# Modulating the Hyena input by feature block over four tiles, the first spectrum on VectorE alone, the gate rows in the last residue, and grouped-query squares on ScalarE

## The chip, the cores and the metric

One core of a Trainium2 chip runs the whole program. The metric is device time in microseconds, median of three runs.

## What is computed

Two layers of a mixer over 1024 sample tokens and 128 prompt tokens of width 1024. The part of the reference that the change touches:

```python
mod = silu(c) @ ada_w + ada_b            # c_ctx for the prompt token tile
shift, scale, gate = split(mod, 3)
h = rmsnorm(x, norm_pre) * (1.0 + scale) + shift
z = h @ w_in                             # 3*256 columns of it are the Hyena input
gq = rmsnorm(g_q, gqa_q_norm); gk = rmsnorm(g_k, gqa_k_norm)   # per head of 64
# Hyena: two long convolutions by real FFT of filters computed by a small sine network
spec = rfft(u, 2n) * rfft(filt, 2n); y = irfft(spec)[:n] + u * bias
out = x + gate * rmsnorm(o @ w_out, norm_post)
```

All is float32.

## The kernel before, in words

Everything is scheduled by hand, engine by engine, with semaphores. A token tile is 128 tokens; tiles 0 to 7 are sample, tile 8 (`NT`) prompt; `TT` is 9. An engine's instructions run in program order. PSUM has eight banks. `claim` (line 671) makes TensorE wait until the last job in a bank was drained; `K.next()` (line 299) deals banks in turn, and `K.restart` sets the turn, so that the turn is not the same in both layers. `full` and `emptied` are the states of a job's bank. An fp32 matmul leaves two records in the trace, a transpose one.

Per layer the stage around the change runs so:

1. For o = 1 and then o = 0, TensorE makes nine filter products (`f3`), then the forward transform in four residues `a0` in `FE_ORDER` (2, 0, 1, 3), two products `p` each, eight jobs `FE`, with the six column blocks of the conditioning (`ada`) laid between. For o = 0 it first makes 16 two-column products (`modT`, one job) that turn the conditioning into columns; behind the residues come four `gate_row` products.
2. ScalarE drains the `FE` jobs into the buffer B2. VectorE (`butterfly`, line 1864) and GpSimd (`butterfly`, line 2496) share the radix-4 step from B2 through B3 to HS: VectorE makes sums and rows 0 and 2, GpSimd the differences and rows 1 and 3. The result for o = 1 goes out by DMA (`spectrum_kept`, line 555), after a wait for GpSimd (line 553). ScalarE drains the `FE` jobs of o = 0 only after the first spectrum is made, since B2 is used again; after some of them it squares a tile of x (`square`, line 1367).
3. VectorE makes the modulation columns (`modulation`, line 1873), normalizes six tiles (`normalize`, line 1892, with an inverse root on GpSimd in its middle), multiplies the gate rows (`gate_rows`), adds the bias, and modulates.
4. TensorE turns x tile by tile (`x_turned`, line 786): two banks of four transposes a tile. ScalarE modulates the lower four feature blocks, VectorE the upper four (`modulate`, line 1899), four instructions of 128 columns each per tile. `hyena_input(f, i)` (line 804) multiplies feature block f by token part i (512, 512 and 128 tokens), eight matmuls each; for f = 0 it waits until all tiles of the part are modulated. Order: tiles 0 to 4, input (0,0), tiles 5 and 6, (1,0), tiles 7 and 8, (0,1), (0,2), and then f = 1 to 5. The ring for x has six places; the DMAs for tiles 6 to 8 start when tiles 0 to 2 are turned.
5. After VectorE made the second spectrum (`butterfly` for o = 0), ScalarE drains the input jobs into the place of B2.

In the grouped-query stage each tile passes through projection (TensorE), a copy to SBUF (ScalarE, line 1765), `head_sums` (VectorE, line 2341: squares, sums, scaled), an inverse root on GpSimd, rotary and `split` (VectorE), and transposes (`parts_turned`, TensorE). The last gate product of the stage goes into bank 7 (line 1299), and the attention's `take_bank` waits for its drain (line 974).

## Time and profile before

| | us |
|---|---|
| median of 3 runs | 2381.16 |
| lowest, highest | 2380.28, 2382.45 |
| the profiled execution | 2381.92 |
| its span | 2380.1 |

TensorE is busy for 93% of the span, VectorE for 55%, ScalarE for 40%, GpSimd for 13%. The mean granted clock of TensorE is 0.993 of full speed. The chain of work that ended last follows the profile back for a few microseconds only, so the order of the work is read from the timelines of the engines, and the idle time before each entry, with what ended it, in brackets. Entries of a timeline merge instructions of the same kind; lengths overlap by some hundredths of a microsecond.

### The profile page before, as it was taken

How to read it: one execution, taken by the hardware profiler on the slowest of the kernel's cores; microseconds unless marked ns; L12 is line 12 of the kernel's file. 1: busy time of each engine (PE TensorE's matmuls, PEld its weight loads, DVE VectorE, ACT ScalarE, POOL GpSimd, SP SyncE). 2: the span in 40 equal slices, each digit the busy share in tenths (PEclk: the TensorE clock that was granted, in tenths of full speed). 3: DMA queues.
4: the chain of work that ended last, by engine and by line, in shares of the span. 5: the costliest groups of instructions: out<-in, count | busy, mean ns of one | idle time of the engine just before them, and what ended most of it. 6: DMA issues, size and time to landing. Idle time of an engine off the chain costs nothing. (4 is left out here: it accounts for less than half of the span.)

```text
span 2380.1 us, 36768 instructions
## 1 busy us (share of the span) xinstructions
PE 2223.0 (93%) x14648; PEld 1605.8 (67%) x14648; DVE 1315.8 (55%) x2450; ACT 961.9 (40%) x1957; POOL 311.3 (13%) x458
## 2 busy tenths in 40 slices
PE   6999999899999998989999999999999999889898
PEld 4556865685677776864866577657856777768657
DVE  3642764564856466583546247545656654855732
ACT  2422113554255266483224221135532652745721
POOL 0410000000200013022314000010011000220323
PEclk9999999999999999999999999999999999999999
DMA  7600100100020000113276001001001100002022
GB/s 238 250 36 29 58 19 1 55 1 15 1 79 2 4 5 7 37 37 134 80 244 238 30 1 58 18 21 35 2 15 38 42 2 7 1 7 73 2 90 88
DMA packets 75042, 124.96 MB, mean 53 GB/s; under 512 B 25778, under 2 KB 38962, under 8 KB 73332
## 3 DMA queue, kind: packets, MB, share of 16 engines
q1 hardware_dynamic: 73816, 121.64, 14.8%
q8 instruction: 118, 1.93, 0.3%
q10 hardware_dynamic: 1056, 0.96, 0.2%
q14 instruction: 52, 0.43, 0.1%
HBM read 105.38 MB, written 17.20 MB: 52 GB/s over the span
## 5 line engine op out<-in xcount | busy, mean ns | idle before, releaser
L677 PE MATMUL psum<-arena 128*32 128x256 f32 (+9 forms) x9168 | 1381.2, 383 | 57.2 <-ACT arena L1352 11.8
L677 PEld LDWEIGHTS psum<-arena 128*32 128x32 f32 (+3 forms) x9168 | 879.5, 149 | 492.2 <-issue 360.0
L681 PE MATMUL psum<-ident,arena 128*128 128x128 f32 (+1 forms) x2248 | 333.3, 278 | 67.5 <-ACT arena L1631 31.1
L1819 DVE TENSOR_TENSOR arena<-arena 128x32 f32<-128x32 f32 (+10 forms) x686 | 307.8, 494 | 102.3 <-ACT arena L1492 42.6
L681 PEld LDWEIGHTS psum<-ident,arena 128*128 128x128 f32 (+1 forms) x2248 | 251.7, 140 | 153.5 <-issue 103.2
L677 PE MATMUL psum<-k_parts,q_parts 96*128 96x384 f32 (+2 forms) x1000 | 267.6, 363 | 11.9 <-ACT arena L1527 6.0
L2113 DVE TENSOR_REDUCE st<-psum 128x1 f32<-128x1152 f32 (+1 forms) x144 | 178.0, 1237 | 48.7 <-PE psum L677 48.4
L2208 DVE TENSOR_REDUCE st<-psum 128x1 f32<-128x1152 f32 (+1 forms) x144 | 174.7, 1236 | 49.0 <-PE psum L677 48.6
L677 PEld LDWEIGHTS psum<-k_parts,q_parts 96*128 96x128 f32 (+1 forms) x1000 | 168.4, 191 | 29.4 <-issue 10.9
L1819 DVE TENSOR_TENSOR arena<-psum,arena 128x512 f32<-128x512 f32 (+2 forms) x104 | 57.1, 564 | 228.1 <-PE psum L677 228.1
L1527 ACT ACTIVATE arena<-psum,st 128x1152 f32<-128x1152 f32 (+1 forms) x144 | 162.4, 1128 | 49.1 <-DVE st L2113 41.4
L1542 ACT COPY arena<-psum 128x512 f32<-128x512 f32 (+1 forms) x244 | 101.9, 433 | 186.1 <-PE psum L681 186.0
L1617 ACT ACTIVATE arena<-psum,st 128x1152 f32<-128x1152 f32 (+1 forms) x144 | 162.3, 1128 | 26.4 <-DVE st L2208 25.4
L2454 POOL TENSOR_TENSOR arena<-arena 128x512 f32<-128x512 f32 (+4 forms) x74 | 135.8, 1846 | 192.2 <-ACT arena L1362 82.5
L2454 POOL TENSOR_TENSOR st<-st,minus 128x1 f32<-128x1 f32 x72 | 42.3, 588 | 721.0 <-ACT arena L1617 721.0
L2127 DVE COPY arena<-psum 128x512 f32<-128x512 f32 (+1 forms) x156 | 93.7, 613 | 28.9 <-PE psum L681 28.9
L1631 ACT COPY arena<-psum 128x512 f32<-128x512 f32 (+1 forms) x200 | 90.2, 469 | 41.5 <-PE psum L681 40.6
L2218 DVE SCALAR_TENSOR_TENSOR arena<-arena,st 128x1152 f32<-128x1152 f32 (+1 forms) x72 | 96.0, 1334 | 11.7 <-POOL st L2454 11.7
L1980 DVE SCALAR_TENSOR_TENSOR arena<-arena,hcw 128x1024 f32<-128x1024 f32 x24 | 30.8, 1285 | 124.2 <-ACT arena L1446 123.8
L2454 POOL TENSOR_TENSOR st<-st,mhalf 128x1 f32<-128x1 f32 (+2 forms) x72 | 60.6, 841 | 242.3 <-DVE st L1824 135.5
L1580 ACT ACTIVATE arena<-psum 128x512 f32<-128x512 f32 x36 | 21.5, 598 | 171.9 <-PE psum L677 171.9
L1741 ACT CAST q_parts<-psum 96x512 fp32r<-96x512 f32 (+1 forms) x54 | 31.5, 584 | 117.8 <-PE psum L681 117.8
(160 smaller groups left out, 1945.6 us busy)
## 6 DMA issues: line engine op xcount, KB each, us to landing
arena<-in_ada_w SPq DMA_DIRECT2D x12, 2048.0 KB, 8.7
arena<-in_w_in SPq DMA_DIRECT2D x10, 2048.0 KB, 8.2
arena<-in_x SPq DMA_DIRECT2D x18, 512.0 KB, 5.7
out_xs<-arena SPq DMA_DIRECT2D x18, 512.0 KB, 2.6
arena<-out_xs SPq DMA_DIRECT2D x18, 512.0 KB, 5.7
arena<-in_w_out SPq DMA_DIRECT2D x4, 2048.0 KB, 8.0
spectrum_kept<-arena SPq DMA_DIRECT2D x2, 2304.0 KB, 8.4
arena<-spectrum_kept SPq DMA_DIRECT2D x2, 2304.0 KB, 8.8
```

Of the source, the lines that this page charges most:

```text
L677: return nc.tensor.matmul(out, lhsT, rhs, start=start, stop=stop)
L681: return nc.tensor.transpose(out, src, ident[0:n, 0:n])
L1527: nc.scalar.activation(at(buf, nk, w), psum[:, 512 * b0:512 * (b0 + nk)].rearrange("p (c n) -> p c n", c=nk)[:, :, 0:w], ACT.Exp, bias=st[ ...
L1542: nc.scalar.copy(at(SLOTS[grp] + slot(grp, u) * 1152 + 512 * j, nk * P), bank[b][:, 0:nk * P]).then_inc(*S.up("turned_scalar", (grp, number)))
L1617: nc.scalar.activation(at(buf, nk, w), psum[:, 512 * b0:512 * (b0 + nk)].rearrange("p (c n) -> p c n", c=nk)[:, :, 0:w], ACT.Exp, bias=st[ ...
L1631: nc.scalar.copy(at(SLOTS[grp] + slot(grp, u) * 1152 + 512 * j, nk * P), bank[b][:, 0:nk * P]).then_inc(*S.up("turned_scalar", (grp, number)))
L1819: return nc.vector.tensor_tensor(out, a, b, op)
L2113: nc.vector.tensor_reduce(st[:, 16 + x % 4:17 + x % 4], psum[:, 512 * b0:512 * (b0 + nk)].rearrange("p (c n) -> p c n", c=nk)[:, :, 0:w], ...
L2127: nc.vector.tensor_copy(at(SLOTS[grp] + slot(grp, u) * 1152 + 512 * j, nk * P), bank[b][:, 0:nk * P]).then_inc(*S.up("turned_vector", (grp ...
L2208: nc.vector.tensor_reduce(st[:, 16 + x % 4:17 + x % 4], psum[:, 512 * b0:512 * (b0 + nk)].rearrange("p (c n) -> p c n", c=nk)[:, :, 0:w], ...
L2218: nc.vector.scalar_tensor_tensor(p0, p1, c, p0, ALU.mult, ALU.add).then_inc(*S.up("mixed", (grp, u)))
L2454: return nc.gpsimd.tensor_tensor(out, a, b, op)
```

## The change

1. The 16 two-column products are laid one by one behind the matmuls of the first two residues of o = 0 (`modulation_column`). The four gate row products move from behind the last residue to between its two products.
2. For o = 1 VectorE makes the whole radix-4 step (`spectrum_butterfly`, eight instructions); GpSimd keeps its part for o = 0 only. The DMA of the spectrum waits for VectorE.
3. Tiles 0 to 3 are turned by feature block: bank k takes block k of all four tiles, and one instruction of 512 columns modulates it (even k ScalarE, odd k VectorE). `hyena_input(0, 0)` waits block by block. Tiles 4, 5 and 6, 7 go in pairs, two blocks to a bank, 256 columns an instruction. Five tiles are normalized before the gate rows, tile 5 after the modulation of the first four, tiles 6 and 7 behind the bias. The DMAs for tiles 6 to 8 all start when the four tiles are turned. Input products take banks 0, 1, 6, 7 where they took 2, 3, 6, 7.
4. In the grouped-query stage ScalarE squares the projection from PSUM between its two copies, and VectorE no longer does. The last gate product takes bank 6.

```diff
@@ -550,7 +551,7 @@
 sp.wait_ge(*K.emptied(("f3", 0, FILTER_ORDER[-1])))
 for t in range(RING):
     load_x(t)
-sp.wait_ge(*S.at("butterfly_pool", ("F", 1)))
+sp.wait_ge(*S.at("spectrum_turned"))
 sp.wait_ge(*S.at("spectrum1_made"))
 sp.dma_start(spectrum_kept, at(HS, 4608)).then_inc(*S.up("spectrum1_kept", None, 16))
@@ -563,7 +564,7 @@
 sp.dma_start(gates_kept, at(SGH, 2 * D)).then_inc(*S.up("gate_rows_kept", None, 16))
 for t in range(RING, TT):
-    sp.wait_ge(*K.full(("xT", t - RING, 1)))
+    sp.wait_ge(*K.full(("xT_four", KD - 1)))
     load_x(t)
 sp.wait_ge(*K.full(("xT", NT, 1)))
 load(at(TI, 4096), I["tab_i"], "inverse_table")
...
@@ -722,6 +723,22 @@
 mod = at(A_MOD, 3072)
+def modulation_column(m, columns):
+    last = mm(columns[:, 2 * m:2 * m + 2], mod[:, m * P:(m + 1) * P], sel[:, :, 0])
+    if m == 2 * KD - 1:
+        last.then_inc(*K.done(("modT",)))
+def gate_row_products():
+    pe.wait_ge(*S.at("ada_biased", 5))
+    for s in range(2):
+        for half in range(2):
+            ps = claim(("gate_row", s, half), K.next())
+            mm(ps[:, :], sel[:, s, :], mod[:, 2 * D + half * 512:2 * D + (half + 1) * 512]
+               ).then_inc(*K.done(("gate_row", s, half)))
 tf = at(TF, 2 * NT, 2, P)
 ti = at(TI, 2 * NT, 2, P)
 eo = at(EO, TT, 3, GW)
...
@@ -766,7 +780,13 @@
                 for i, (a, kind) in enumerate(terms):
                     last = mm(ps[:, ri * GW:(ri + 1) * GW], tf[:, 2 * a + p, ri, :],
                               eo[:, a, kind, :], i == 0, i == len(terms) - 1)
+                    if o == 0 and turn < 2 and (ri, i) != (1, len(terms) - 1):
+                        modulation_column(8 * turn + 4 * p + 2 * ri + i, columns)
             last.then_inc(*K.done(("FE", o, a0, p)))
+            if o == 0 and turn < 2:
+                modulation_column(8 * turn + 4 * p + 3, columns)
+            if o == 0 and (turn, p) == (3, 0):
+                gate_row_products()
         if turn == 1:
             pe.wait_ge(*S.at("filter_folded", (o, NT)))
             ps = claim(("FEp", o), K.next())
@@ -775,13 +795,26 @@
             last.then_inc(*K.done(("FEp", o)))
     if o:
         ada(3)
-    else:
-        pe.wait_ge(*S.at("ada_biased", 5))
-        for s in range(2):
-            for half in range(2):
-                ps = claim(("gate_row", s, half), K.next())
-                mm(ps[:, :], sel[:, s, :], mod[:, 2 * D + half * 512:2 * D + (half + 1) * 512]
-                   ).then_inc(*K.done(("gate_row", s, half)))
+def four_turned():
+    for t in FOUR:
+        pe.wait_ge(*S.at("x_normed", t))
+    for k in range(KD):
+        ps = claim(("xT_four", k), [k])
+        for t in FOUR:
+            last = flip(ps[:, t * P:(t + 1) * P], at(XN[t] + k * P, P))
+        last.then_inc(*K.done(("xT_four", k)))
...
+def pair_turned(n, banks):
+    for t in PAIRED[n]:
+        pe.wait_ge(*S.at("x_normed", t))
+    for j in range(4):
+        ps = claim(("xT_pair", n, j), banks[j])
+        for i in range(2):
+            for a, t in enumerate(PAIRED[n]):
+                last = flip(ps[:, (2 * i + a) * P:(2 * i + a + 1) * P],
+                            at(XN[t % RING] + (2 * j + i) * P, P))
+        last.then_inc(*K.done(("xT_pair", n, j)))
 def x_turned(t, banks):
...
@@ -805,25 +838,27 @@
     c, (tok, n) = "hy0" if f < 4 else "hy1", PARTS[i]
     weights(c)
-    if f < 1:
-        for t in range(tok // P, (tok + n) // P):
-            for half in range(2):
-                pe.wait_ge(*K.emptied(("xT", t, half)))
+    if f < 1 and i == 1:
+        for pair in range(2):
+            for j in range(4):
+                pe.wait_ge(*K.emptied(("xT_pair", pair, j)))
+    if f < 1 and i == 2:
+        for half in range(2):
+            pe.wait_ge(*K.emptied(("xT", NT, half)))
     ps = claim(("u", f, i), banks)
     for k in range(KD):
+        if f < 1 and i == 0:
+            pe.wait_ge(*K.emptied(("xT_four", k)))
         last = mm(ps[:, 0:n], W[:, SLOT[c, 0], k, (f % 4) * P:(f % 4 + 1) * P],
                   hT[:, k, tok:tok + n], k == 0, k == KD - 1)
     last.then_inc(*K.done(("u", f, i)))
-for t in range(4):
-    x_turned(t, ([2 * t], [2 * t + 1]))
-x_turned(4, ([0], [1]))
-hyena_input(0, 0, [2])
-x_turned(5, ([4], [5]))
-x_turned(6, ([6], [7]))
-hyena_input(1, 0, [3])
-x_turned(7, ([0], [1]))
-x_turned(8, ([4], [5]))
+four_turned()
+hyena_input(0, 0, [0])
+pair_turned(0, ([2], [3], [4], [5]))
+hyena_input(1, 0, [1])
+pair_turned(1, ([6], [7], [2], [3]))
+x_turned(NT, ([4], [5]))
 hyena_input(0, 1, [6])
...
@@ -971,7 +1006,7 @@
         for j in range(pieces(grp, u)):
             turned_by[piece_number(grp, u, j)] = f"turned_{piece_engine(grp, u, j)}"
-    side = {7: K.emptied(("gate", "gqa", *LAST_GATE["gqa"]))} if grp == "gqa" else {}
+    side = {6: K.emptied(("gate", "gqa", *LAST_GATE["gqa"]))} if grp == "gqa" else {}
     def take_bank(b, released):
@@ -1296,7 +1331,7 @@
     parts_turned(grp, TT)
     if grp == "gqa":
         gate("gqa", "gqa_gate", 0, *GQA_GATES[4], K.next())
-    gate(grp[:4], vg, vg0, *LAST_GATE[grp], [7])
+    gate(grp[:4], vg, vg0, *LAST_GATE[grp], [6 if grp == "gqa" else 7])
     if grp != "diff1":
         pe.wait_ge(*S.at(f"{grp[:4]}_values"))
...
-                                    bias=mcol[:, k, s:s + 1])
-    last.then_inc(*K.drained(job))
-    if t >= 3 and t + 3 < TT:
-        square(t + 3)
+def modulate(job, k, s, tok, c, n):
+    return nc.scalar.activation(hT[:, k, tok:tok + n], B(job)[:, c:c + n], ACT.Identity,
+                                scale=mcol[:, KD + k, s:s + 1], bias=mcol[:, k, s:s + 1])
+for k in range(0, KD, 2):
+    act.wait_ge(*K.full(("xT_four", k)))
+    modulate(("xT_four", k), k, 0, 0, 0, 512).then_inc(*K.drained(("xT_four", k)))
+square(6)
+square(7)
+for n in range(2):
+    for j in range(2):
+        job = ("xT_pair", n, j)
+        act.wait_ge(*K.full(job))
+        modulate(job, 2 * j, 0, 512 + n * 256, 0, 256)
+        modulate(job, 2 * j + 1, 0, 512 + n * 256, 256, 256).then_inc(*K.drained(job))
+    if n == 0:
+        square(8)
+job = ("xT", NT, 0)
+act.wait_ge(*K.full(job))
+for k in range(4):
+    last = modulate(job, k, 1, NT * P, k * P, P)
+last.then_inc(*K.drained(job))
 act.wait_ge(*S.at("butterfly_vector", ("F", 0)))
...
@@ -1764,6 +1812,10 @@
             nz = 384 if grp == "gqa" else 256
             ins = nc.scalar.copy(at(z, nz), B(job)[:, 0:nz])
             if grp == "gqa":
+                if i >= 1:
+                    act.wait_ge(*S.at("variance", ("heads", i - 1)))
+                nc.scalar.activation(at(SQ, 384), B(job)[:, 0:384], ACT.Square)
                 ins = nc.scalar.copy(at(VV + key_tile(i) * GW, P), B(job)[:, 384:512])
             ins.then_inc(*K.drained(job))
         if grp == "gqa" and i + GQA_SPLIT + 1 < TT:
...
@@ -1870,6 +1922,19 @@
     tt(X[:, 0, :], M[:, 0, :], M[:, 1, :], ALU.add)
     link(tt(X[:, 2, :], M[:, 0, :], M[:, 1, :], ALU.subtract), "butterfly_vector", key)
+def spectrum_butterfly(src, mid, dst):
+    E, M, X = at(src, 4, D), at(mid, 4, D), at(dst, 4, D)
+    R, Y = at(mid, 4, 2, 2, GW), at(dst, 4, 2, 2, GW)
+    link(tt(M[:, 0:2, :], E[:, 0:2, :], E[:, 2:4, :], ALU.add), "butterfly_sums", ("F", 1))
+    link(tt(M[:, 2:4, :], E[:, 0:2, :], E[:, 2:4, :], ALU.subtract), "spectrum_diffs")
+    tt(X[:, 0, :], M[:, 0, :], M[:, 1, :], ALU.add)
+    tt(X[:, 2, :], M[:, 0, :], M[:, 1, :], ALU.subtract)
+    tt(Y[:, 1, :, 0, :], R[:, 2, :, 0, :], R[:, 3, :, 1, :], ALU.add)
+    tt(Y[:, 1, :, 1, :], R[:, 2, :, 1, :], R[:, 3, :, 0, :], ALU.subtract)
+    tt(Y[:, 3, :, 0, :], R[:, 2, :, 0, :], R[:, 3, :, 1, :], ALU.subtract)
+    link(tt(Y[:, 3, :, 1, :], R[:, 2, :, 1, :], R[:, 3, :, 0, :], ALU.add), "spectrum_turned")
 def modulation():
...
+def modulate_four():
+    for k in range(1, KD, 2):
+        v.wait_ge(*K.full(("xT_four", k)))
+        modulate(("xT_four", k), k, 0, 0, 0, 512).then_inc(*K.drained(("xT_four", k)))
+def modulate_pair(n):
+    for j in range(2, 4):
+        job = ("xT_pair", n, j)
+        v.wait_ge(*K.full(job))
+        modulate(job, 2 * j, 0, 512 + n * 256, 0, 256)
+        modulate(job, 2 * j + 1, 0, 512 + n * 256, 256, 256).then_inc(*K.drained(job))
+def modulate_prompt():
+    job = ("xT", NT, 1)
     v.wait_ge(*K.full(job))
     for k in range(4):
-        last = nc.vector.tensor_scalar(hT[:, 4 + k, t * P:(t + 1) * P], B(job)[:, k * P:(k + 1) * P],
-                                       mcol[:, KD + 4 + k, s:s + 1], mcol[:, 4 + k, s:s + 1],
-                                       ALU.mult, ALU.add)
+        last = modulate(job, 4 + k, 1, NT * P, k * P, P)
     last.then_inc(*K.drained(job))
...
@@ -1936,9 +2018,12 @@
 for o in (1, 0):
     if o == 0:
         modulation()
-        for t in range(RING):
+        for t in range(RING - 1):
             normalize(t)
         gate_rows()
+        v.wait_ge(*K.emptied(("gate_row", 1, 1)))
+        modulate_four()
+        normalize(RING - 1)
     for a0 in range(4):
         for p in range(2):
...
@@ -1949,13 +2034,17 @@
         link(nc.vector.scalar_tensor_tensor(E[:, 0, p, 0, :], bias, 1.0 / N_SAMPLE, E[:, 0, p, 0, :],
                                             ALU.mult, ALU.add), "bias_added", (o, p))
     if o == 0:
-        v.wait_ge(*K.emptied(("gate_row", 1, 1)))
-        for t in range(TT):
-            modulate(t)
-            if t >= 4 and t + 2 < TT:
-                normalize(t + 2)
+        normalize(6)
+        normalize(7)
+        modulate_pair(0)
+        normalize(8)
+        modulate_pair(1)
+        modulate_prompt()
         v.wait_ge(*S.at("spectrum1_kept"))
-    butterfly(("F", o), B2, B3, HS, -1)
+    if o:
+        spectrum_butterfly(B2, B3, HS)
+    else:
+        butterfly(("F", o), B2, B3, HS, -1)
     v.wait_ge(*K.emptied(("FEp", o)))
     nc.vector.scalar_tensor_tensor(at(HS + 4096, GW), bias, 1.0 / N_PROMPT, at(B2 + 4096, GW),
...
@@ -2341,8 +2430,7 @@
 def head_sums(i):
     v.wait_ge(*K.emptied(("proj", "gqa", i)))
-    z, r6 = ZB + (i % 2) * WC, st[:, 8 * (i % 2):8 * (i % 2) + 6]
-    link(tt(at(SQ, 384), at(z, 384), at(z, 384), ALU.mult))
+    r6 = st[:, 8 * (i % 2):8 * (i % 2) + 6]
     link(nc.vector.tensor_reduce(r6, at(SQ, 6, 64), AX.X, ALU.add))
     nc.vector.tensor_scalar(r6, r6, 1.0 / 64, EPS, ALU.mult, ALU.add).then_inc(*S.up("variance", ("heads", i)))
...
@@ -2531,13 +2619,12 @@
             inverse_root(("x", t), st[:, t:t + 1])
             if t == 1:
                 bias_ada(5)
-    for a0 in range(4):
-        for p in range(2):
-            pool.wait_ge(*K.emptied(("FE", o, a0, p)))
-    pool.wait_ge(*S.at("bias_added", (o, 1)))
-    if o == 0:
-        pool.wait_ge(*S.at("spectrum1_kept"))
-    butterfly(("F", o), B2, B3, HS, -1, range(RING, TT) if o == 0 else ())
+for a0 in range(4):
+    for p in range(2):
+        pool.wait_ge(*K.emptied(("FE", 0, a0, p)))
+pool.wait_ge(*S.at("bias_added", (0, 1)))
+pool.wait_ge(*S.at("spectrum1_kept"))
+butterfly(("F", 0), B2, B3, HS, -1, range(RING, TT))
```

## Rows read from the trace of the kernel before

**Rows 1.** The page, first part: busy time, share of the span and instructions of each engine.

```profile
PE 2223.0 (93%) x14648; PEld 1605.8 (67%) x14648; DVE 1315.8 (55%) x2450; ACT 961.9 (40%) x1957; POOL 311.3 (13%) x458
```

**Rows 2.** Waits of TensorE over the whole span: who waited for whom, us, times, longest.

```profile
PE psum L681 <- DVE split_buf L1819: 8.7, 10, 1.2
```

**Rows 3.** Timeline of TensorE, layer 0: start us, us, engine, line, operation, idle before it.

```profile
69.85 3.73 PE L677 MATMUL psum<-sel,arena 128*128 128x2 f32 x32
...
73.45 13.52 PE L677 MATMUL psum<-arena 128*128 128x256 f32 x68
...
88.10 10.63 PE L677 MATMUL psum<-arena 128*128 128x256 f32 x48 [1.13 <-DVE mcol L1879]
...
98.56 3.60 PE L677 MATMUL psum<-arena,sel 128*128 128x512 f32 x8
...
102.00 3.66 PE L681 MATMUL psum<-ident,arena 128*128 128x128 f32 x32
...
110.66 9.81 PE L677 MATMUL psum<-arena 128*128 128x512 f32 x16 [3.37 <-DVE arena L1904]
...
122.06 7.03 PE L677 MATMUL psum<-arena 128*128 128x512 f32 x16
...
131.62 17.54 PE L677 MATMUL psum<-arena 128*128 128x512 f32 x64 [0.78 <-DVE arena L1904]
```

**Rows 4.** Timeline of TensorE, layer 1, the same stage.

```profile
1246.25 25.40 PE L677 MATMUL psum<-arena 128*128 128x256 f32 x116
...
1276.27 4.88 PE L681 MATMUL psum<-ident,arena 128*128 128x128 f32 x40 [1.18 <-DVE arena L1819]
...
1283.59 8.74 PE L677 MATMUL psum<-arena 128*128 128x512 f32 x16 [2.44 <-DVE arena L1904]
...
1303.47 8.89 PE L677 MATMUL psum<-arena 128*128 128x512 f32 x32 [0.78 <-DVE arena L1904]
...
1314.99 8.89 PE L677 MATMUL psum<-arena 128*128 128x512 f32 x32 [2.63 <-ACT arena L1439]
```

**Rows 5.** Windows: length, busy us of five engines, granted clock, DMA share, GB/s.

```profile
1246.20:1250.00 3.80, 3.80 (x11) 3.12 (x12) 3.73 (x5) 0.95 (x3) 1.98 (x1) 0.59 0.44 117
...
113.00:116.00 3.00, 3.00 (x5) 1.09 (x4) 1.91 (x2) 2.67 (x8) 1.78 (x2) 0.50 0.14 53
```

**Rows 6.** Timeline of VectorE, layer 0.

```profile
75.24 9.96 DVE L1819 TENSOR_TENSOR arena<-arena 128x2048 f32<-128x2048 f32 x3
...
91.52 0.76 DVE L1896 TENSOR_SCALAR arena<-arena,st 128x1024 f32<-128x1024 f32 x1 [0.67 <-POOL st L2454]
...
101.92 2.48 DVE L1819 TENSOR_TENSOR arena<-psum,arena 128x512 f32<-128x512 f32 x4
...
127.23 1.75 DVE L1896 TENSOR_SCALAR arena<-arena,st 128x1024 f32<-128x1024 f32 x1 [0.66 <-POOL st L2454]
...
132.56 4.68 DVE L1819 TENSOR_TENSOR arena<-arena 128x2048 f32<-128x2048 f32 x3
```

**Rows 7.** Timeline of GpSimd, layer 0.

```profile
75.38 14.97 POOL L2454 TENSOR_TENSOR arena<-arena 128x2048 f32<-128x2048 f32 x6 [10.94 <-DVE arena L1949]
```

**Rows 8.** Timeline of ScalarE, layer 0.

```profile
92.06 0.61 ACT L1411 ACTIVATE arena<-psum 128x512 f32<-128x512 f32 x1
...
112.09 1.06 ACT L1371 ACTIVATE arena<-arena 128x1024 f32<-128x1024 f32 x1 [1.92 <-DMA arena<-in_x]
```

**Rows 9.** Timeline of TensorE, grouped-query stage of layer 0.

```profile
594.02 0.47 PE L677 MATMUL psum<-gqa_w_high,gqa_h_high 128*128 128x512 f32 x1 [1.50 <-DVE gqa_w_low L1819]
...
614.65 1.09 PE L681 MATMUL psum<-ident,split_buf 128*128 128x128 f32 x8 [0.77 <-DVE split_buf L1819]
...
669.68 2.02 PE L677 MATMUL psum<-arena 128*128 128x128 f32 x16 [0.98 <-ACT k_parts L1749]
```

**Rows 10.** Timeline of VectorE, grouped-query stage of layer 0.

```profile
614.51 0.55 DVE L1819 TENSOR_TENSOR arena<-arena 128x384 f32<-128x384 f32 x1
```

**Rows 11.** Timeline of ScalarE, grouped-query stage of layer 0.

```profile
616.35 0.49 ACT L1765 COPY arena<-psum 128x384 f32<-128x384 f32 x1
```

19 lines of the change are left out of this document (6 added, 13 removed).

## Prediction

> **What bounds the kernel now.** The page's busy line comes first: TensorE is busy for 93% of the span, nobody else for more than 55% [rows 1]. So a change is worth what it takes out of TensorE's idle time, what it gives back of TensorE's clock, and nothing else; work moved between the other engines counts only where TensorE waits for it. The second view is therefore TensorE's timeline through the stage, with the wait in brackets, once per layer [rows 3, 4]. The reader sees a queue that runs without a gap through the filter transform and then breaks up: it waits 1.13 us for the modulation columns in layer 0 and 1.18 us for a drained gate row in layer 1, 3.37 and 2.44 us for the modulation of the first four tiles, 0.78 us for that of the last ones, and in layer 1 another 2.63 us for a bank that ScalarE has to drain. The third view is the windows with the granted clock [rows 5]: two places of this stage run at or near 1.2 GHz and not 2.4. Last come VectorE, GpSimd and ScalarE at the same times [rows 6 to 8], to see what is late next, and the same three views in the grouped-query stage [rows 2, 9 to 11].
>
> **First spectrum on VectorE alone.** Before, VectorE's three instructions take 9.96 us while GpSimd's six run for 14.97 us beside them [rows 6, 7]; the same three take 4.68 us where GpSimd is silent at 132.56 [rows 6]. The new eight instructions are the 2048-column sum twice, two of 1024 columns and four of 512. The old three are one sum and two of 1024, so four units of 1024 columns took 4.68 us: 1.17 us a unit. The new work is eight units, 9.4 us, with GpSimd silent. The two small copies behind it also ran beside GpSimd before. I expect the first spectrum 2 to 2.5 us sooner (bounds 0 to 3), and the columns with it. TensorE reaches the bank of the columns at 86.97 (73.45 + 13.52) and waits 1.13 us [rows 3]: that wait goes. In layer 1 there was none, as TensorE was slower there by the clock. Two DMAs of weights and one of the spectrum start about 3.4 us sooner, since GpSimd's end is no longer awaited. Gain: 1.1 us, layer 0.
>
> **Columns laid into the residues.** The 16 products took 3.73 us for 32 records [rows 3], 0.117 us each, which is a weight load and not the two columns. Laid between matmuls of 256 columns each still brings two weight loads, of which one at most hides behind its neighbour. I put the change at nothing, bounds -1.9 and +1.9 us a layer. What it may change is the clock. In layer 1 the 3.8 us right behind the block of columns were granted 0.59, so mostly 1.2 GHz [rows 5], and the 116 records took 25.40 us where layer 0 took 13.52 + 10.63 = 24.15 [rows 3, 4]. What TensorE did before it fell was a stretch of 32 weight loads with almost no columns; spread out, there is no such stretch. I take 1.25 us back in layer 1 (bounds 0 and 1.25).
>
> **Gate rows in the last residue.** The same 3.60 us of TensorE [rows 3], free of cost, but VectorE's 2.48 us for the gate rows [rows 6] now runs beside the last product instead of behind everything. The 1.18 us wait in layer 1 [rows 4] was for a gate row's bank; by counting the banks dealt, in layer 1 the gate rows now hold 6, 7, 0, 1 and the last product 2, all drained when the turned block reaches them. By walking the queues VectorE ends the gate rows about 0.8 us before the last product ends: cover enough, and without it up to 1 us a layer comes back. The gate rows wait for the last conditioning block, which GpSimd completes behind its second inverse root; walking the queues puts that about 2 us early.
>
> **Four tiles by block.** The 32 transposes take 3.66 us [rows 3], 0.114 us each, so a block of four is full every 0.46 us. An engine drains one in about 0.61 us (ScalarE) or 0.62 us (VectorE, 2.48 / 4) [rows 6, 8], and each gets every second block, one in 0.92 us: the engines keep up. The first input product uses a block every 7.03 / 8 = 0.88 us [rows 3], so it can start right behind the transposes. Before, it stood behind 40 transposes and the 3.37 us wait, and then ran at 1.2 GHz: the window shows 0.50, and the product took 9.81 us, not 7.03 [rows 3, 5]. In layer 1: 2.44 us and 8.74 us [rows 4].
>
> New TensorE line from the start of the transposes to input (0,1): 32 transposes 3.6, product 6.9, 16 transposes 1.8, product 6.9, 16 and 8 transposes 2.8, together 22.0 us, start to start. I add 0.5 us for the last modulation, as VectorE must normalize tile 8 and modulate two banks before (0,1). That makes 22.5. Before it was 131.62 - 102.00 = 29.62 us in layer 0 [rows 3]: gain 7.1. In layer 1 it was 1303.47 - 1276.27 = 27.20 [rows 4]: gain 4.7, and with the 1.18 us wait and the 1.25 us of clock 7.1. Layer 0 with its 1.1 us makes 8.2.
>
> **What is late next.** Tile 6 must be normalized before the second pair is turned, 19.2 us into the new line (3.6 + 6.9 + 1.8 + 6.9). Its DMA landed at 112.0 before (ScalarE waited 1.92 us for it [rows 8]); that is 11 us into the new line, and the queue ahead of it starts 3.4 us sooner. Squares of tiles 6 and 7 take 1.06 us each. Normalizing costs VectorE 0.76 us alone and 1.75 us beside GpSimd's part of the second spectrum [rows 6]. With 1.75 each and GpSimd's root between, both are done about 17.3 us into the line. Cover: 1.9 us. ScalarE now has its squares ahead of the first pair's modulation, which no transposed bank is short of.
>
> **The bank in layer 1.** The 2.63 us wait at 1314.99 [rows 4] is input (1,1) claiming bank 3, which input (1,0) held. Now (1,0) takes bank 1 and bank 3 holds a turned pair long drained. The wait goes. In layer 0 (1,1) now claims bank 0 with input (0,0) in it, undrained until the second spectrum is made; the same walk has that due about 1.6 us before. Gain 2.6 us in layer 1 (bounds 1 and 2.6). Behind this stage TensorE's queue has no gap that depends on an absolute time, so the shift stays.
>
> **Grouped-query squares.** Per tile TensorE waits 0.77 us for VectorE's split [rows 9], ten such waits of 8.7 us in all [rows 2]. VectorE's loop runs without slack but for the root, and it loses one instruction of 0.55 us [rows 10], 0.59 with its gap. Five waits a layer; the stage's first wait, 1.50 us for the rounded weights [rows 9], shrinks by 0.2 only, as ScalarE now squares before it lets VectorE go. VectorE's shift grows by 0.59 a tile and TensorE takes it over but for about 0.2 us that remains a tile: 4.35 - 1.2 = 3.1 us a layer, 6.3 in all (bounds 0 and 8.7). ScalarE's new instruction is like its copy, 0.49 us [rows 11], and ScalarE idles for over 3 us in each tile. It waits for the variance of the tile before, which VectorE makes right behind the split whose transposes ScalarE drains first: no wait, and only this tile's two copies would be queued behind it.
>
> **Last gate in bank 6.** Bank 7 held the last transposed keys, and TensorE waited 0.98 us [rows 9]; bank 6 was drained a tile ago. Twice 0.98: 2.0 us.
>
> **Sum.** 8.2 + 7.1 + 2.6 + 6.3 + 2.0 = 26.2 us. The profiled execution had 2381.92 us around its span of 2380.1, so it would have 2355.7; it lies 0.76 above the median of 2381.16, which gives 2355.0.
>
> **A rule beside the rows.** VectorE's three instructions took twice as long beside GpSimd [rows 6, 7]. The Trainium skill (SBUF — State Buffer, Who interferes with whom) says that a VectorE instruction with two SBUF inputs, or one in a two-port mode, and a GpSimd instruction lock each other out for a whole instruction. By that rule, the trace agrees, the new spectrum is safe, but the normalizing of tiles 6 to 8 is not: it now stands in the middle of GpSimd's second spectrum. That is the third rival below.
>
> **The rivals.**
> *Transposes cool the clock* (15%). The 32 transposes in a row are 3.66 us of short work, and both falls of the clock came near short work. Against it: the clock was still full during them. Then the first product costs 8.74 to 9.81 us as now, +1.7 to +2.8 us in both layers: about 2359.5.
> *The squares were not the bound* (8%). ScalarE's longer drain takes the place of VectorE's instruction: none of the 6.3 us, 2361.3.
> *VectorE late for the tail* (12%). Each of tiles 6 to 8 waits for one more GpSimd instruction. A 512-column one is some 1.3 us (14.97 us holds the 2048-column one, four such and a small one, slowed); three are 3.9 us, and the 0.5 us at input (0,1) grows by all of it: +7.8 us over two layers, 2362.8.
> *The clock is lost over the whole stage* (3%, the one that ends slower). Thin products in the residues and short transposes keep TensorE at 1.2 GHz, where work takes twice as long. The two residues with columns are 10.6 us of work, the transposes and first product 10.5. If all of that ran slow in both layers it costs 42 us: 2397. It decides from 13.1 us of slow work a layer. Against it: layer 0 ran the densest block of columns and what followed with no fall at all.
>
> **How the numbers follow.** The forecast holds 62%, its own range 2351 to 2358. With the second to fourth cases up to 2363 no more than 2 in 10 are left out. Below, 2350 takes in TensorE losing all waits for the split and hidden column loads in part. A difference of 0.2% (4.8 us) is about what a measurement of this kernel can tell from no change. Every case but the last is faster by more: 0.95; 0.02 for a sum of mishaps within it, 0.03 slower.
>
> **What would show it.** After: no wait for the columns; transposes x32 followed at once by the first product in 7.03 us at a clock of 1.0; input (0,1) 22.5 us behind the first transpose; no wait for ScalarE's drain in front of (1,1) in layer 1; VectorE's first spectrum in 9 to 9.5 us; waits for the split down from 8.7 to about 2.4 us; none of 0.98 us before the last gate. Wrong would be a wait of over 1 us for a normalized tile, a first product of over 8 us, or a per-tile wait for the split still near 0.77.

## The result and the profile after

| | before | after |
|---|---|---|
| median, us | 2381.8 (2380.28 to 2386.9) | 2358.14 (2356.43 to 2358.81) |
| the profiled execution | 2381.92 | 2357.67 |
| its span | 2380.1 | 2355.9 |
| mean granted clock | 0.993 | 0.993 |

The ratio of the changed kernel to the one before, on one chip, is 0.9892 with a 95% interval of 0.988 to 0.9905: about 1.1% faster, 2358.14 us where 2355.0 was forecast.

The page first, as before: busy time, share and instructions of each engine. TensorE is busy for 4.5 us less than in [rows 1], with as many instructions; the other 20 us of the 24.2 us of span are idle time that went.

```profile
PE 2218.5 (94%) x14648; PEld 1604.3 (68%) x14648; DVE 1295.3 (55%) x2402; ACT 959.2 (41%) x1935; POOL 281.4 (12%) x448
```

TensorE's timeline in layer 0 (start us, us, engine, line, operation, idle before it). It answers [rows 3]. The 80.02 row is the last of the 16 two-column products, each between two records of 128x256.

```profile
80.02 0.28 PE L678 MATMUL psum<-sel,arena 128*128 128x2 f32 x2
80.16 13.52 PE L678 MATMUL psum<-arena 128*128 128x256 f32 x68
93.52 3.60 PE L678 MATMUL psum<-arena,sel 128*128 128x512 f32 x8
96.95 3.62 PE L678 MATMUL psum<-arena 128*128 128x256 f32 x16
100.40 3.66 PE L682 MATMUL psum<-ident,arena 128*128 128x128 f32 x32
103.89 7.03 PE L678 MATMUL psum<-arena 128*128 128x512 f32 x16
...
112.51 7.03 PE L678 MATMUL psum<-arena 128*128 128x512 f32 x16
119.38 2.92 PE L682 MATMUL psum<-ident,arena 128*128 128x128 f32 x24
123.21 17.54 PE L678 MATMUL psum<-arena 128*128 128x512 f32 x64 [0.91 <-DVE arena L1966]
```

No column wait stands inside the 68 records, the gate rows stand ahead of the last 16 records of the transform, the 32 transposes are followed by the first product at once, and this takes 7.03 us where it took 9.81. From the first transpose to input (0,1) it is 123.21 - 100.40 = 22.81 us, where it was 29.62. One wait is left, 0.91 us.

The same stage in layer 1, answering [rows 4]: again 1287.53 - 1264.68 = 22.85 us, where it was 27.20, and 64 records in one row where the wait for ScalarE had cut them into 32 and 32.

```profile
1264.68 3.69 PE L682 MATMUL psum<-ident,arena 128*128 128x128 f32 x32
1268.21 7.03 PE L678 MATMUL psum<-arena 128*128 128x512 f32 x16
...
1287.53 17.54 PE L678 MATMUL psum<-arena 128*128 128x512 f32 x64 [0.91 <-DVE arena L1966]
```

Windows over the first product of layer 0 and over what follows the columns in layer 1 (length, busy us of five engines, granted clock, DMA share, GB/s). Where [rows 5] show 0.50 and 0.59, both are now at the upper level, 2.4 GHz:

```profile
104.00:111.00 7.00, 7.00 (x20) 3.12 (x19) 2.57 (x7) 2.62 (x5) 4.12 (x2) 1.00 0.95 372
1244.50:1248.30 3.80, 3.80 (x26) 1.88 (x25) 3.77 (x5) 0.00 (x0) 0.00 (x0) 1.00 1.02 419
```

VectorE, GpSimd and ScalarE in layer 0, the same columns as the timeline of TensorE; these rows answer [rows 6 to 8]:

```profile
75.75 9.42 DVE L1871 TENSOR_TENSOR arena<-arena 128x2048 f32<-128x2048 f32 x8
...
105.63 0.75 DVE L1961 TENSOR_SCALAR arena<-arena,st 128x1024 f32<-128x1024 f32 x1 [0.66 <-POOL st L2542]
...
112.63 1.75 DVE L1961 TENSOR_SCALAR arena<-arena,st 128x1024 f32<-128x1024 f32 x1 [2.29 <-POOL st L2542]
...
115.11 1.75 DVE L1961 TENSOR_SCALAR arena<-arena,st 128x1024 f32<-128x1024 f32 x1 [0.67 <-POOL st L2542]
...
119.39 1.76 DVE L1961 TENSOR_SCALAR arena<-arena,st 128x1024 f32<-128x1024 f32 x1 [0.67 <-POOL st L2542]
121.07 3.17 DVE L1966 TENSOR_SCALAR arena<-psum,mcol 128x256 f32<-128x256 f32 x8
```

```profile
107.43 4.53 POOL L2542 TENSOR_TENSOR arena<-arena 128x2048 f32<-128x2048 f32 x1 [1.84 <-DVE arena L2034]
112.04 0.55 POOL L2542 TENSOR_TENSOR st<-st,mhalf 128x1 f32<-128x1 f32 x1
```

```profile
108.93 1.06 ACT L1406 ACTIVATE arena<-arena 128x1024 f32<-128x1024 f32 x1 [4.02 <-DMA arena<-in_x]
```

The first spectrum takes 9.42 us for its eight instructions. The x tile 6 is there at 108.9, 3.1 us sooner than at 112.0 before. Its inverse root on GpSimd (112.04) stands behind GpSimd's first instruction of the second spectrum, 4.53 us from 107.43 on, so VectorE waits 2.29 us for it, and VectorE's normalizing takes 1.75 us beside GpSimd, where that of tile 5 took 0.75 with GpSimd silent (105.63).

Waits of TensorE in both grouped-query stages (who waited for whom, us, times, longest), answering [rows 2] and the first of [rows 9]:

```profile
PE psum L682 <- DVE split_buf L1871: 2.0, 6, 0.4
...
PE psum L678 <- DVE gqa_w_low L1871: 2.6, 2, 1.3
```

**Where the 24 us went.** Starts of the same instruction, before and after, give the gain of each stage:

| stage | forecast | measured, two layers |
|---|---|---|
| Hyena, layer 0, to input (0,1) | 8.2 | 8.2 (1.4 ahead of the transposes, 6.8 behind) |
| Hyena, layer 1, to input (0,1) | 7.1 | 7.4 (3.0 ahead, 4.4 behind) |
| bank before input (1,1), layer 1 | 2.6 | 2.9 |
| grouped-query squares | 6.3 | 7.8 |
| last gate | 2.0 | 2.5 |
| sum | 26.2 | 28.8 |
| span | | 24.2 |

Every term came at its size or above it, and yet the span fell by 24.2 us only. The missing 4.6 us stand outside all changed stages. Below are the windows at one of the places where the shift of the two traces jumps, here by 1.7 us: first of the changed kernel, then of a second profiled execution of the same kernel (experiment 1).

```profile
770.00:775.00 5.00, 3.85 (x46) 2.43 (x36) 1.76 (x7) 1.16 (x5) 0.00 (x0) 0.92 0.00 0
775.00:780.00 5.00, 5.00 (x19) 4.13 (x19) 0.00 (x0) 0.23 (x1) 0.00 (x0) 0.74 0.01 3
```

```profile
770.00:775.00 5.00, 3.85 (x43) 2.50 (x35) 1.76 (x7) 1.16 (x5) 0.00 (x0) 1.00 0.00 0
775.00:780.00 5.00, 5.00 (x25) 4.38 (x24) 0.00 (x0) 0.27 (x1) 0.00 (x0) 1.00 0.02 3
```

TensorE was busy to the same extent in both up to 775; in the one its clock fell, and in the next 5 us it did 19 records where the other did 25.

**The bracket is not the whole price of a wait.** Three terms came above their waits, and starts show why. In a queue that runs, neighbouring records overlap: the transposes above end at 100.40 + 3.66 = 104.06, and the product starts at 103.89. A wait takes this overlap of 0.16 us away, and the second record behind it comes another 0.03 to 0.10 us late. So the bracket of 0.98 us before the last gate [rows 9] was worth 1.24 us of start to start, that of 1.13 us for the columns [rows 3] 1.4, and that of 2.63 us for the bank [rows 4] 2.9.

### The profile page after: what moved, and what is told of

The parts are those of the page before. It is cut to its first block and busy times, and to the rows that moved or that the text cites. A ratio compares the mean times of both kernels' runs of the same rounds, so it can differ in the third digit from the quotient of the medians.

```text
span 2355.9 us, 36664 instructions
## 1 busy us (share of the span) xinstructions
PE 2218.5 (94%) x14648; PEld 1604.3 (68%) x14648; DVE 1295.3 (55%) x2402; ACT 959.2 (41%) x1935; POOL 281.4 (12%) x448
## 5 line engine op out<-in xcount | busy, mean ns | idle before, releaser
L1871 DVE TENSOR_TENSOR arena<-arena 128x256 f32<-128x256 f32 (+9 forms) x678 | 298.4, 487 | 84.4 <-ACT arena L1540 42.6
L2542 POOL TENSOR_TENSOR arena<-arena 128x512 f32<-128x512 f32 (+4 forms) x64 | 108.9, 1710 | 177.9 <-ACT arena L1397 95.1
L2307 DVE SCALAR_TENSOR_TENSOR arena<-arena,st 128x1152 f32<-128x1152 f32 (+1 forms) x72 | 96.0, 1334 | 11.8 <-POOL st L2542 11.8
```

Of the source, the lines that this page charges most:

```text
L1871: return nc.vector.tensor_tensor(out, a, b, op)
L2307: nc.vector.scalar_tensor_tensor(p0, p1, c, p0, ALU.mult, ALU.add).then_inc(*S.up("mixed", (grp, u)))
L2542: return nc.gpsimd.tensor_tensor(out, a, b, op)
```

## The experiments

Two measures are used. The median is that of four executions, of ten in experiments 10 and 11. Experiments 1 to 4, 5 to 8 and 9 to 11 ran on three different chips; each ratio is to the kernel before on the same chip, so a ratio compares better across these groups than a median. Beside it stands the profiled span *at full clock*, an estimate: the lost clock is the sum over all 5-us windows of 5 us x (1 - granted clock), and 0.85 of it is taken off the span. The 0.85 comes from two pairs of executions of an identical kernel: spans of 2355.9 and 2351.3 us with 17.1 and 11.8 us lost, and of 2380.1 and 2385.4 with 18.6 and 25.2. It gives 2341.4 and 2341.3 for the one pair, 2364.3 and 2363.9 for the other, where the spans themselves differ by 5 us. That these agree tests nothing, since the 0.85 was taken from them; the timelines of the experiments below do, and differ from the number by up to 2 us. So a part worth 1 to 5 us, which the medians can't tell, is read from the timeline, with this number beside it.

| kernel | median, us | ratio to before | span at full clock | against changed |
|---|---|---|---|---|
| before | 2381.8 | 1 | 2364.3 | +22.9 |
| changed | 2358.14 | 0.9892 | 2341.4 | |
| 1 changed, again | 2356.01 | 0.9888 (0.9871 to 0.9904) | 2341.3 | -0.1 |
| 2 squares on VectorE | 2365.87 | 0.992 (0.9906 to 0.9935) | 2349.1 | +7.7 |
| 3 bank 3 for (1,0) | 2360.41 | 0.9901 (0.9886 to 0.9916) | 2344.6 | +3.2 |
| 4 columns in a block | 2358.05 | 0.9892 (0.9877 to 0.9907) | 2341.2 | -0.2 |
| 5 tile by tile | 2373.81 | 0.9949 (0.9933 to 0.9966) | 2357.5 | +16.1 |
| 6 gate rows last | 2355.34 | 0.9871 (0.9857 to 0.9886) | 2340.8 | -0.6 |
| 7 spectrum shared | 2357.85 | 0.988 (0.9866 to 0.9895) | 2342.7 | +1.3 |
| 8 last gate in bank 7 | 2357.58 | 0.9884 (0.9869 to 0.9899) | 2344.2 | +2.8 |
| 9 blocks waited for together | 2359.42 | 0.9901 (0.9883 to 0.9918) | 2343.5 | +2.1 |
| 10 part 4 alone | 2379.02 | 0.9981 (0.9969 to 0.9992) | 2353.7 | -10.6 against before |
| 11 before, again | 2386.49 | 1.0004 (0.9992 to 1.0016) | 2363.9 | -0.4 against before |

### 1. The changed kernel again: what are the falls of the clock in the attention?

The theory: the missing 4.6 us are falls that come or stay away from one execution to the next. The rival: the change moved the work so that they come always. No edit.

> The changed kernel once more, unaltered. What is to be told apart: the stages of the change gave back 8.3, 7.5 and 3.1 us in and behind the modulation of layers 0 and 1 and 10.2 us in the two grouped-query stages, 29 in all, but the span fell by 24.2 us; the other 5 us went in the attention stages, in steps of 1.7 us each, at each of which the windows show a granted clock of about 0.5. Theory A (the falls come by chance of phase and move from execution to execution): here the falls outside the changed stages stand at other times than 255, 420, 770, 910, 1060, 1420, 2220, their number differs by one to three, and the time is 2355 to 2360. Theory B (the change itself causes them): they stand at the same places in the same number.

The falls near 420, 770, 1060 and 1420 us are gone and a new one stands at 1580; those near 255, 910, 2220 and 2350 are there again. 11.8 us of clock were lost and not 17.1, and the span is 2351.3 us, 4.6 shorter, of the same kernel. The second span is 28.8 us below that of before, which is the 28.8 of the table. So the gain was made, and in the first profile part of it was covered by falls that need not have come. The rival is answered by the kernel before: its second execution (experiment 11) has falls at 425, 1070 and 1445 us, at the same instructions as those at 420, 1060 and 1420 here, though its first had none of them. But the theory holds in half only. Whether a fall comes changes from one execution to the next; where it can come is much the same in all thirteen traces, as the last section tells.

### 2. The squares back on VectorE

```diff
-                nc.scalar.activation(at(SQ, 384), B(job)[:, 0:384], ACT.Square)
...
+    link(tt(at(SQ, 384), at(z, 384), at(z, 384), ALU.mult))
```

> The changed kernel with the grouped-query squares back on VectorE. My theory: VectorE's loop sets the pace again, each grouped-query stage is 3.9 us longer (I forecast 3.1), waits for the split return to about 8.7 us in all, the time is 6 to 8 us above the changed kernel. Rival (TensorE's own work or ScalarE's drain was the bound, the gain came from the bank of the last gate): under 1 us.

TensorE's waits, as above:

```profile
PE psum L682 <- DVE split_buf L1867: 8.8, 10, 1.3
```

Ten waits of 8.8 us are back where the changed kernel has six of 2.0, and the median rises by 7.7 to 9.9 us over the two medians of the changed kernel. The squares were the bound, and the forecast's 6.3 for this term was too small.

### 3. Input (1,0) in bank 3 again

```diff
-pair_turned(0, ([2], [3], [4], [5]))
-hyena_input(1, 0, [1])
-pair_turned(1, ([6], [7], [2], [3]))
+pair_turned(0, ([2], [1], [4], [5]))
+hyena_input(1, 0, [3])
+pair_turned(1, ([6], [7], [2], [1]))
```

> The changed kernel with banks 1 and 3 exchanged in the Hyena input: input (1,0) sits in bank 3, a turned pair in bank 1. My theory: in layer 1 TensorE waits again before input (1,1) for ScalarE to drain (1,0), 2.6 to 3.1 us, in layer 0 nowhere; the time is 2.6 to 3.1 us above the changed kernel. Rival (the wait went because ScalarE's drain comes earlier, whichever bank): no wait, same time.

TensorE in layer 1, the product of input (1,1):

```profile
1297.32 10.59 PE L678 MATMUL psum<-arena 128*128 128x512 f32 x32 [2.91 <-ACT arena L1487]
```

The wait of [rows 4] is back with 2.91 us (2.63 before), in layer 1 alone; by the starts it costs 3.1 us. Behind it the records took 10.59 us where 32 of them take 8.89: the granted clock was 0.80 in the window from 1295 and 0.85 in that from 1300, so in this execution a fall of the clock stood beside the wait.

### 4. The 16 columns in one block

```diff
+for m in range(2 * KD):
+    modulation_column(m, columns)
...
-                    if o == 0 and turn < 2 and (ri, i) != (1, len(terms) - 1):
-                        modulation_column(8 * turn + 4 * p + 2 * ri + i, columns)
```

> The changed kernel with the 16 two-column products in one block ahead of the residues, as before. My theory: at equal clock the stretch from the first residue to the transposes is within 0.5 us of the changed kernel's 30.6 us; where the clock falls behind the block, as in layer 1 before, it is 1.2 to 1.7 us longer. Rival (laid between, half of the weight loads hide): 1.9 us longer in both layers at a clock of 1.0.

TensorE in layer 0 and in layer 1, and the windows behind the block in layer 1:

```profile
70.06 3.73 PE L678 MATMUL psum<-sel,arena 128*128 128x2 f32 x32
```

```profile
1232.97 4.17 PE L678 MATMUL psum<-sel,arena 128*128 128x2 f32 x32
1237.00 23.35 PE L678 MATMUL psum<-arena 128*128 128x256 f32 x100
```

```profile
1235.00:1240.00 5.00, 5.00 (x23) 4.46 (x23) 4.90 (x9) 1.67 (x4) 0.38 (x1) 0.61 0.07 10
1240.00:1245.00 5.00, 5.00 (x18) 4.11 (x18) 4.93 (x3) 0.00 (x0) 0.00 (x0) 0.71 0.98 373
```

In layer 0 the way from the first of these records to the transposes is 100.80 - 70.06 = 30.74 us. Laid between it is 30.74 us too, from the first record behind the filter products at 69.66 us to 100.40: the columns cost the same in either place. In layer 1 the clock falls right behind the block, as in [rows 5], and the same way takes 34.1 us: 3.4 more, where at most 1.7 was expected. The medians are alike all the same; 3.4 us are within what executions of one kernel differ by. What is shown is the equal price. That spreading the columns *keeps* the clock rests on a count: a fall stands right behind the block of layer 1 in all four traces that have one there (before, before again, experiment 10 and this one), and in none of the nine with the columns spread.

### 5. Turned and modulated tile by tile

`x_turned` for all nine tiles, four modulations of 128 columns a tile and engine, six tiles normalized before the gate rows, the DMAs for tiles 6 to 8 and banks 2 and 3, all as before; the rest as changed.

```diff
-four_turned()
-hyena_input(0, 0, [0])
+for t in range(4):
+    x_turned(t, ([2 * t], [2 * t + 1]))
+x_turned(4, ([0], [1]))
+hyena_input(0, 0, [2])
...
-        for t in range(RING - 1):
+        for t in range(RING):
```

> The changed kernel with the turning and modulation undone: tile by tile, 128 columns an instruction, the old order of normalizing and the old banks 2 and 3; all else stays changed. My theory: the stretch from the first transpose to input (0,1) goes from 22.8 us back to 27 to 30 in both layers, with a wait of 2.4 to 3.4 us before the first product and a fall of the clock in it, and input (1,1) of layer 1 waits 2.6 to 3 us for its bank: 14 us above the changed kernel, about 2371. Rival (with the gate rows and the spectrum sooner, the tile order alone costs little): under 5 us.

TensorE in both layers, and VectorE in layer 1:

```profile
104.49 4.93 PE L682 MATMUL psum<-ident,arena 128*128 128x128 f32 x28 [2.62 <-DVE arena L1836]
112.50 7.11 PE L678 MATMUL psum<-arena 128*128 128x512 f32 x16 [3.08 <-DVE arena L1934]
...
130.75 4.53 PE L678 MATMUL psum<-arena 128*128 128x512 f32 x10 [0.78 <-DVE arena L1934]
```

```profile
1272.82 7.42 PE L682 MATMUL psum<-ident,arena 128*128 128x128 f32 x40 [5.21 <-DVE arena L1836]
```

```profile
1269.31 0.15 DVE L1841 TENSOR_SCALAR st<-st 128x1 f32<-128x1 f32 x1 [4.72 <-ACT arena L1384]
...
1270.80 2.48 DVE L1836 TENSOR_TENSOR arena<-psum,arena 128x512 f32<-128x512 f32 x4
```

The way from the first transpose to input (0,1) is 130.75 - 100.40 = 30.35 us in layer 0, where it is 22.81 with blocks. In layer 1 the same way takes 26.5 us where it is 22.85, behind a wait of 5.21 us, and the bank wait of 2.63 us is back too, since (1,0) is in bank 3 again: 7.5 + 8.9 + 2.6 = 19.0 us, some 4 to 5 of them clock (0.71 granted at 105, 0.69 and 0.63 at 1270 and 1275 us). The medians are 15.7 and 17.8 us above those of the changed kernel, the ratio 0.9949 where it was 0.9892: by far the largest part, where 14 was expected. The wait of 5.21 us has a mechanism of its own: VectorE waits 4.72 us for the square of tile 5, which ScalarE makes only behind the last residue, and drains the gate rows after that (1270.80). Their banks are full as long, and TensorE waits 5.21 us for one. With the gate rows moved forward and the sixth tile left in front of them, their wait, 1.18 us in layer 1 before [rows 4], becomes one of 2.62 us in layer 0 and of 5.21 in layer 1. So by this trace, normalizing five tiles and not six ahead of the gate rows is a needed half of the change. No run has that half alone, so the 14 to 19 us are not shared out between the tile order and the order of normalizing.

### 6. The gate rows behind the last residue

```diff
-            if o == 0 and (turn, p) == (3, 0):
-                gate_row_products()
...
+    else:
+        gate_row_products()
```

> The changed kernel with the gate rows behind the last residue. My theory: in layer 1 the turned blocks 0 and 1 wait for banks that hold gate rows, 1.2 to 2 us, in layer 0 nothing up to 0.7 us: 1 to 3 us in all. Rival (the place of the gate rows does not matter, as the banks are drained in time): no new wait, same time.

VectorE in layer 1, the first and the last of four such rows, then its first modulation:

```profile
1259.11 0.69 DVE L1871 TENSOR_TENSOR arena<-psum,arena 128x512 f32<-128x512 f32 x1 [0.48 <-PE psum L678]
...
1261.69 0.69 DVE L1871 TENSOR_TENSOR arena<-psum,arena 128x512 f32<-128x512 f32 x1 [0.17 <-PE psum L678]
1262.64 3.49 DVE L1966 TENSOR_SCALAR arena<-psum,mcol 128x512 f32<-128x512 f32 x4 [0.26 <-PE psum L682]
```

My theory fell. I had VectorE drain four gate rows in a row of 2.48 us behind the last product; it drains each in 0.69 us while the next, 0.86 us apart, is made, so that only the last one is late, and the first modulation takes up its work 0.26 us after that. The transposes wait for nothing, and from them to input (0,1) it is 22.93 us, as against 22.85. Moving the gate rows into the residue is worth nothing, once VectorE comes to them in time; 2355.34 us is the lowest median of all, but no more below 2356.01 than the same kernel differs from itself.

### 7. The first spectrum shared with GpSimd again

```diff
-    if o:
-        spectrum_butterfly(B2, B3, HS)
-    else:
-        butterfly(("F", o), B2, B3, HS, -1)
+    butterfly(("F", o), B2, B3, HS, -1)
...
```

GpSimd's half and the waits of the DMA and of ScalarE for it are back too.

> The changed kernel with GpSimd sharing the first spectrum again. My theory: the modulation columns come 2.3 us later, so TensorE waits 1 to 1.5 us for them in both layers now (in layer 1 the fallen clock hid it before), x for tiles 6 to 8 lands 3 us later and is still covered: 2 to 3 us in all. Rival (the later DMAs are not covered, tiles 6 and 7 are normalized too late): 5 us or more. Other rival (nothing is waited for): 0.

TensorE in both layers, and VectorE's spectrum and the two small operations behind it in layer 0:

```profile
88.14 7.17 PE L678 MATMUL psum<-arena 128*128 128x256 f32 x32 [1.12 <-DVE mcol L1944]
```

```profile
1253.45 7.17 PE L678 MATMUL psum<-arena 128*128 128x256 f32 x32 [1.12 <-DVE mcol L1944]
```

```profile
75.28 9.96 DVE L1871 TENSOR_TENSOR arena<-arena 128x2048 f32<-128x2048 f32 x3
85.28 1.37 DVE L2046 SCALAR_TENSOR_TENSOR arena<-arena 128x256 f32<-128x256 f32 x1
86.58 1.35 DVE L2048 COPY arena<-arena 128x256 f32<-128x256 f32 x1
```

The wait of 1.13 us for the columns [rows 3] is back, and in layer 1 too, where TensorE is now as fast as in layer 0. By the starts each costs 1.4 us, 2.8 in all, of which the span at full clock shows 1.3. VectorE has fewer instructions and needs longer, 9.96 us, and 1.37 and 1.35 us for two operations that take 0.42 and 0.29 alone. Half the step given to another engine was no relief at all.

### 8. The last gate in bank 7 again

```diff
-gate(grp[:4], vg, vg0, *LAST_GATE[grp], [6 if grp == "gqa" else 7])
+gate(grp[:4], vg, vg0, *LAST_GATE[grp], [7])
...
```

> The changed kernel with the last gate product of the grouped-query stage in bank 7 again. My theory: a wait of 1.0 us for the last transposed keys returns in both layers, 2.0 to 2.4 us in all. Rival (it hides behind the first scores' own wait for ScalarE): 0.

TensorE in layer 0:

```profile
657.75 2.02 PE L678 MATMUL psum<-arena 128*128 128x128 f32 x16 [0.98 <-ACT k_parts L1797]
```

The wait of [rows 9] is back at its old size, 0.98 us in each layer, though the instruction itself comes 12 us sooner than before. From the second record behind it on, everything is 1.21 us late: 2.4 us in two layers, with 2.8 by the span at full clock.

### 9. Input (0,0) waits for all eight blocks

```diff
+    if f < 1 and i == 0:
+        for k in range(KD):
+            pe.wait_ge(*K.emptied(("xT_four", k)))
```

(and the wait inside the loop over k goes).

> The changed kernel, but input (0,0) waits for all eight turned blocks and not block by block. It parts the two halves of the gain before the first product. My theory (both count): the last block is drained 0.7 to 0.9 us after the last transpose, so that much idle time and no fall of the clock per layer, 1.4 to 1.8 us in all. Rival (the wide instructions alone do it): 0. Other rival (the wait by block is the main part): over 3 us and a fallen clock in the first product, as before.

TensorE, the first product in layer 0 and in layer 1:

```profile
105.26 7.11 PE L678 MATMUL psum<-arena 128*128 128x512 f32 x16 [1.21 <-ACT arena L1454]
```

```profile
1271.23 7.10 PE L678 MATMUL psum<-arena 128*128 128x512 f32 x16 [1.20 <-DVE arena L1967]
```

It waits 1.2 us in each layer, where 0.7 to 0.9 was expected, and then runs in 7.11 us at full clock; by the starts each wait costs 1.45 us, 2.9 in all. This splits the gain behind the transposes: of 3.37 and 2.44 us of wait [rows 3, 4], 1.2 are saved by waiting block by block. The rest comes with the blocks themselves, eight instructions of 512 columns instead of 32 of 128 for the four tiles, and with no fifth tile turned and no sixth normalized ahead of the product; these are not told apart. The wait of 1.2 us ahead of the product did not bring its clock down, and neither did one of 3.08 us in layer 0 of experiment 5 (112.50, 7.11 us), though there the clock had fallen at 105. In the kernel before it fell in this product, behind 3.37 and 2.44 us.

### 10. Part 4 alone, in the kernel before; 11. the kernel before again

The squares on ScalarE and the last gate in bank 6, laid into the kernel before. The second run is that kernel unaltered, on the same chip.

```diff
+                if i >= 1:
+                    act.wait_ge(*S.at("variance", ("heads", i - 1)))
+                nc.scalar.activation(at(SQ, 384), B(job)[:, 0:384], ACT.Square)
...
-    link(tt(at(SQ, 384), at(z, 384), at(z, 384), ALU.mult))
```

> The kernel before with the grouped-query part alone: squares on ScalarE and the last gate in bank 6. My theory (the parts add up, since each takes a wait of TensorE in its own stage): 7.8 + 2.0 to 2.4 = about 10 us under the kernel before, 2371 to 2374. Rival (part of it comes only with the change of the earlier stage): under 7 us.

> The kernel before, unaltered, for its falls of the clock outside the changed stages. If they come by chance they stand at other times than 265, 1600, 2095, 2245 and 2375 of the first look, up to three more or fewer; the time is 2380 to 2387. If they belong to the kernel, the same places.

```profile
PE psum L681 <- DVE split_buf L1823: 2.1, 6, 0.4
...
PE psum L677 <- DVE gqa_w_low L1823: 2.6, 2, 1.3
```

The waits went as in the changed kernel, and in layer 0 the work behind the stage came 5.2 us sooner (3.98 by the squares and the wait for the weights, 1.2 by the gate). But the medians are only 7.5 us apart (2379.02 and 2386.49), and the one stands 5.4 below the median of 19 executions of the kernel before on that chip, so the 2371 to 2374 were missed, and the medians alone would not exclude the rival of under 7 us. What lies between is clock. The profiled execution lost 27.1 us of it, the unaltered kernel 25.2, that of [rows 1] 18.6, and at full clock the one is 10.6 us below the other, near the 7.8 + 2.5 of the table. It is not an accident of one profile: over ten executions each the mean granted clock is 0.9889 with part 4 and 0.9909 without, and the span at full clock worked out from them differs by 10.2 us. So the waits were saved, and part of the gain went into a lower clock. Why this kernel is granted less than the one before is not shown.

The second profile of the kernel before answers its own question in the same way: outside the changed stages four of the five falls of the first profile came again near the same instructions, that at 265 us did not, and four are new, near 425, 670, 1070 and 1445 us.

## Why the prediction was right, and where it was not

**First spectrum, columns.** 9.4 us were forecast for the eight instructions and 9.42 were measured; the modulation columns came 2.1 us sooner, within the 2 to 2.5. The wait of 1.13 us went. But experiment 7 puts the part at 2.8 us in two layers and not at the 1.1 of the sum. Before, the columns of layer 1 were in time only because TensorE was slow there; at full clock it would have waited 1.12 us, which costs 1.4. So the 1.25 us that the sum got from spreading the columns needed this part as well.

**Two-column products between the residues.** The nothing, with bounds of 1.9 us each way, was nothing: 30.74 us either way (experiment 4). The clock in layer 1, forecast at 1.25 us, came back as 1.6: the 3.0 us ahead of the transposes less 1.4 for the wait of 1.18. The block itself had been slow in part (3.90 us and not 3.73). In experiment 4 it is 3.4: what a fall costs is not fixed.

**Gate rows.** Forecast as free and without a wait; so it was. But the step gave the reason to the wrong part: by experiment 6 the place in the residue isn't needed. By experiments 5 and 6 the 1.18 us hung on when VectorE gets to the gate rows: where it gets there late, there are 5.21 us, and where it is in time, none.

**Four tiles by block.** The forecast line of 22.5 us was 22.81 and 22.85. Each element of it holds: 3.5 us for 32 transposes (100.40 to 103.89), 6.9 for a product, 1.75 for 16 transposes. The 0.5 us for the last modulation was 0.91: tile 8 was normalized in 1.76 us beside GpSimd, and the last pair's modulation stands behind it (121.07). It cost 0.4 us a layer. The first rival, transposes that cool the clock, didn't come in any profile of a kernel with blocks.

**VectorE late for the tail.** The third rival was partly there: tile 6's root waited for one GpSimd instruction, 2.29 us. It cost nothing, as tiles 6 and 7 were normalized at 116.86 and TensorE turned them at 119.38. The cover was 2.5 us, 1.9 in the forecast. Each tile cost VectorE 1.75 us beside GpSimd's work and 0.75 without it (105.63). The Trainium skill (SBUF — State Buffer, Who interferes with whom) says that a VectorE instruction in a two-port mode and a GpSimd instruction lock each other out; the trace agrees, in the price and in its place.

**The bank.** 2.6 forecast, 2.9 measured and 3.1 by experiment 3, in layer 1 alone, with no wait for bank 0 in either layer, as the walk of the queues said.

**Grouped-query squares.** This is the term that was mis-sized: 3.1 us a layer forecast, 3.9 measured. Two things make the difference. The sum took 1.2 us off for the remainders, where five of 0.2 us are 1.0, and left out the 0.2 us by which the wait for the weights shrinks; with both, its own terms give 3.5, and the brackets agree (three waits of 1.1 us in all are left of five of 4.3). The other 0.4 us is the lost overlap of two waits that went altogether. VectorE's turn shows the same gain. It took 614.65 - 607.30 = 7.35 us a tile before and takes 611.44 - 598.14 = 13.30 us for two tiles now, 0.70 us less for each and not 0.59, since its wait of 0.61 us for GpSimd's root is gone as well. The fourth mechanism named, ScalarE queued behind the variance, did not show. A smaller one did, VectorE waiting for ScalarE's rounding of the next tile:

```profile
605.90 1.30 DVE L1871 TENSOR_TENSOR gqa_h_low<-arena,gqa_h_high 128x512 fp32r<-128x512 f32 x2 [0.77 <-ACT gqa_h_high L1616]
```

```profile
598.14 1.09 PE L682 MATMUL psum<-ident,split_buf 128*128 128x128 f32 x8 [0.36 <-DVE split_buf L1871]
...
611.44 1.09 PE L682 MATMUL psum<-ident,split_buf 128*128 128x128 f32 x8 [0.36 <-DVE split_buf L1871]
```

VectorE runs on without a gap from there to the split that TensorE waits 0.36 us for at 611.44, so this wait is part of what is left. **Last gate:** 2.0 forecast, 2.5 measured, 1.96 of it the two brackets and the rest the lost overlap.

**"So the shift stays."** This step failed. The sum held the clock to be a matter of the changed stages. In those it was right: 5.74 us were forecast to come back (1.25, 2.78 and 1.71), and as the kernel gains 22.9 us at full clock, some 6 us of the 28.8 are clock. But in the rest of the program, where no instruction of TensorE changed, the clock falls for some 1.7 us at a time, and which falls come is not the same in two executions. The changed kernel's profile lost 4.6 us of the gain to it, its second profile none. The 2355.0 lies between the two profiled executions of the same kernel (2357.67 and 2353.1), so the forecast's error is no larger than what two executions differ by.

That the total came so near is luck in part. The stages gave 2.6 us more than the sum and the clock elsewhere took 4.6 us, which offset each other; the terms alone would have been off by 2.6 us the other way. And 2358.14 us is 0.14 us above the 2351 to 2358 that the forecast gave to its own case, though inside the 2350 to 2363 of the whole.
